# Sums of squares of the input norm taken by TensorE instead of VectorE, in a kernel of two transformer-like blocks

## The reference

```python
def rmsnorm(x, w):
    xf = x.astype(jnp.float32)
    xf = xf * lax.rsqrt(jnp.mean(xf * xf, axis=-1, keepdims=True) + EPS)
    return (xf * w.astype(jnp.float32)).astype(x.dtype)

def hybrid_layer(x, p_i, norm_pre, ...):
    h = rmsnorm(x, norm_pre)
    proj = h @ w_in
    ...
    gate = jax.nn.sigmoid(x @ w_ple_gate)
    return x + gate * (p_i @ w_ple_proj)
```

## Time and profile before

| | |
|---|---|
| runs | 2607.85, 2612.5, 2614.89 us |
| span of the profiled execution, first to last instruction | 2605.7 us |
| TensorE matmuls busy | 2510.6 us, 96% |
| VectorE busy | 1361.5 us, 52% |
| ScalarE busy | 633.4 us, 24% |
| GpSimd busy | 1034.6 us, 40% |
| mean granted clock of TensorE | 0.985 |

### The profile page before, as it was taken

The page is one execution under the profiler, slowest core; times in us unless marked ns, Lnnn a source line. Parts: engine busy times, 40 slices in busy tenths (PEclk is TensorE's granted clock), DMA queues, the critical chain, the costliest instruction groups (busy, mean ns, idle before and its releaser), DMA issues.

```text
span 2605.7 us, 34941 instructions
## 1 busy us (share of the span) xinstructions
PE 2510.6 (96%) x13322; PEld 2056.9 (79%) x13322; DVE 1361.5 (52%) x1592; ACT 633.4 (24%) x714; POOL 1034.6 (40%) x467
## 2 busy tenths in 40 slices
PE   7999999999999799999999999999899999999996
PEld 5778888887888588778778787888678888888885
DVE  6765565556511751223366666556845435445357
ACT  4332232222201211350122222221421111111113
POOL 4443433343433643233222332334444444444441
PEclk9999999998999899999999999999899999999998
DMA  5112222122111321122212222221011111111111
GB/s 197 49 58 73 73 80 73 64 89 81 41 48 60 110 89 59 64 101 77 93 62 74 78 69 73 85 97 48 25 49 49 49 48 48 48 48 49 48 49 65
DMA packets 77307, 178.40 MB, mean 68 GB/s; under 512 B 8225, under 2 KB 34081, under 8 KB 76210
## 3 DMA queue, kind: packets, MB, share of 16 engines
q1 hardware_dynamic: 36288, 119.55, 13.8%
q10 hardware_dynamic: 40946, 57.78, 6.5%
HBM read 149.98 MB, written 27.33 MB: 68 GB/s over the span
## 4 chain that ended last, share of the span: by engine, by line
PE 84%; DVE 8%; issue 3%; DMA 2%; ACT 2%; POOL 1%; ACTq 0%; DVEq 0%; POOLq 0%
PE pt L1486 71%; PE pt L1516 2%; PE pt L1502 2%; DMA eb<-o_d 1%; PE wk L1783 1%; DVE eb L1324 1%; PE wk L1641 1%; PE wk L1553 1%; PE wk L1642 1%; PE wk L1753 1%; PE wk L1818 1%; PE wk L1817 1%; PE wk L1541 1%; PE wk L1822 1%; PE wk L1705 0%
## 5 line engine op out<-in xcount | busy, mean ns | idle before, releaser
L351 POOL TENSOR_TENSOR w_hi<-w_raw,ones 128x1024 fp32r<-128x1024 f32 x202 | 390.3, 1932 | 1468.6 <-PE pt L1486 1403.5
L355 POOL TENSOR_TENSOR w_lo<-w_raw,w_hi 128x1024 fp32r<-128x1024 f32 x202 | 588.3, 2912 | 15.8
L1486 PE MATMUL pt<-h,w_hi 128*128 128x512 f32 x1376 | 439.6, 401 | 8.6 <-POOL w_lo L355 4.6
L1486 PE MATMUL pt<-l,w_hi 128*128 128x512 f32 x1376 | 426.2, 391 | 0.0
L1486 PE MATMUL pt<-h,w_lo 128*128 128x512 f32 x1376 | 425.3, 390 | 0.0
L1486 PE MATMUL pt<-xh,w_hi 128*128 128x512 f32 x976 | 305.6, 395 | 7.3 <-POOL w_lo L355 4.8
L1486 PEld LDWEIGHTS pt<-l,w_hi 128*128 128x128 f32 x1376 | 259.3, 188 | 55.7
L1486 PEld LDWEIGHTS pt<-h,w_lo 128*128 128x128 f32 x1376 | 258.9, 188 | 55.5
L1486 PE MATMUL pt<-xh,w_lo 128*128 128x512 f32 x976 | 302.7, 392 | 0.0
L1486 PEld LDWEIGHTS pt<-h,w_hi 128*128 128x128 f32 x1376 | 250.6, 189 | 64.2 <-issue 6.3
L1486 PE MATMUL pt<-xl,w_hi 128*128 128x512 f32 x864 | 269.0, 393 | 0.0
(11 more groups left out here) (355 smaller groups left out, 3314.1 us busy)
## 6 DMA issues: line engine op xcount, KB each, us to landing
w_raw<-ws_d SPq DMA_DIRECT2D x204, 512.0 KB, 3.4
x_raw<-xT_d SPq DMA_DIRECT2D x32, 256.0 KB, 7.4
rowb<-acs_d ACTq DMA_DIRECT2D x8, 1024.0 KB, 4.6
qkc<-qk_d ACTq DMA_DIRECT2D x9, 512.0 KB, 3.9
pp_d<-ebuf ACTq DMA_DIRECT2D x8, 512.0 KB, 3.3
sz_d<-eb ACTq DMA_DIRECT2D x8, 512.0 KB, 2.6
eb<-pp_d ACTq DMA_DIRECT2D x8, 512.0 KB, 4.2
qk_d<-ebuf ACTq DMA_DIRECT2D x8, 512.0 KB, 2.7
```

The source lines that it names most:

```text
L351: nc.gpsimd.tensor_tensor(out=w_hi[:, u, :], in0=w_raw[:, u, :], in1=zeros, op=ALU.add).then_inc(w_hi_done, 1)
L355: nc.gpsimd.tensor_tensor(out=w_lo[:, u, :], in0=w_raw[:, u, :], in1=w_hi[:, u, :].bitcast(f32), op=ALU.subtract).then_inc(w_split, 1)
L1486: ins = MM(pt[:, slot, h * HALF:(h + 1) * HALF], wt[:, w, k * P:(k + 1) * P], x[:, k, h * HALF:(h + 1) * HALF], start=first and k == 0 and ...
```

## The change

TensorE now sums the squares themselves, without VectorE. For each half tile q it makes four matmuls with a quarter of the squares as the stationary operand and the column of ones as the moving one, and the 8 tiles of a half accumulate in the same four columns of PSUM (bank 3 of wk for the first half, bank 2 for the second). Squares lie in six buffers: four in the space of acc_a and acc_b, and the two in ec. ScalarE waits for a buffer only from the seventh square on. The groups of four matmuls are spread over the PLE tiles: q = 0 to 3 ahead of tile 0, then 4 and 5, 6 and 7, 8 to 10, 11 to 13, 14, and 15 behind tiles 0 to 5. The spread of the first half stands behind tile 2, that of the second half behind tile 7, ahead of the projection. The last group of a half is followed by a wait of TensorE for first_acc (or sq_used), then it raises stat_done. ScalarE's table of steps and VectorE's order are new; VectorE's adds and copies are gone.

```diff
--- before.py
+++ after.py
@@ -138,6 +138,7 @@
     x_raw = at("x_raw", [KT, T], R1)
     p_raw, p_hi, p_lo = at("p_raw", [2, T], R2), at("p_hi", [2, T], R3, f32r), at("p_lo", [2, T], R3 + 8192, f32r)
     acc_a, acc_b = at("acc_a", [1024], BC), at("acc_b", [1024], BC + 4096)
+    xsq = at("xsq", [4, HALF], BC)
     acc_g = at("acc_g", [2, 1024], R3 + 24576)
 
     raw_p = at("raw_p", [2, T + CW], R2 + 8192)
@@ -230,6 +231,10 @@
     def cols(h):
 
         return slice(h * HALF, (h + 1) * HALF)
+
+    def x_square(q):
+
+        return xsq[:, q % 6, :] if q % 6 < 4 else ec[:, cols(q % 6 - 4)]
 
     def sem(name):
         return ctx.enter_context(nc.semaphore(name))
@@ -415,11 +420,9 @@
 
             h, k = divmod(q, KT)
             act.wait_ge(x_in[h][k], 16)
-            if q in (KT, KT + 1):
-                act.wait_ge(first_acc, q - 1)
-            elif q >= 2:
-                act.wait_ge((first_acc, sq_used)[h], k - 1)
-            A(ec[:, cols(q % 2)], x_raw[:, k, cols(h)], ACT.Square).then_inc((first_sq, sq_done)[h], 1)
+            if q >= 6:
+                act.wait_ge(*((first_acc, q - 5) if q < 14 else (sq_used, q - 13)))
+            A(x_square(q), x_raw[:, k, cols(h)], ACT.Square).then_inc((first_sq, sq_done)[h], 1)
 
         def embedding(k):
 
@@ -436,10 +439,10 @@
             act.wait_ge((half_val, val_done)[h], k + 1)
             A(xh[:, k, cols(h)], x_raw[:, k, cols(h)], ACT.Copy).then_inc((half_hi, hi_done)[h], 1)
 
-        for step, first, end in ((square, 0, 4), (embedding, 0, 1), (square, 4, 6), (embedding, 1, 2), (square, 6, 8),
-                                 (embedding, 2, 3), (square, 8, 10), (embedding, 3, 4), (square, 10, 12),
-                                 (embedding, 4, 5), (high, 0, 3), (square, 12, 14), (embedding, 5, 6), (high, 3, 5),
-                                 (square, 14, 16), (embedding, 6, 7), (high, 5, 8), (embedding, 7, 8)):
+        for step, first, end in ((square, 0, 6), (embedding, 0, 1), (square, 6, 8), (embedding, 1, 2), (square, 8, 11),
+                                 (embedding, 2, 3), (square, 11, 14), (embedding, 3, 4), (high, 0, 2), (square, 14, 16),
+                                 (embedding, 4, 5), (high, 2, 4), (embedding, 5, 6), (high, 4, 6), (embedding, 6, 7),
+                                 (high, 6, 8), (embedding, 7, 8)):
             for q in range(first, end):
                 step(q)
         for q in range(KT, 2 * KT):
@@ -869,23 +872,13 @@
         for k in range(2):
             dve.wait_ge(p_hi_done, k + 1)
             TT(out=p_lo[:, k, :], in0=p_raw[:, k, :], in1=p_hi[:, k, :].bitcast(f32), op=ALU.subtract).then_inc(p_lo_done, 1)
-        def half_scale(h, n):
+        def half_scale(h, n, sums=3):
 
             dve.wait_ge(stat_done, n)
             a, b = 4 * h, 4 * h + 4
-            link(TS(sm[:, 8 + a:8 + b], wk[:, 3, a:b], 1.0 / D, EPS1, ALU.mult, ALU.add))
+            link(TS(sm[:, 8 + a:8 + b], wk[:, sums, a:b], 1.0 / D, EPS1, ALU.mult, ALU.add))
             rsqrt(sm[:, a:b], sm[:, 8 + a:8 + b], sm[:, 16 + a:16 + b], rstd_done)
 
-
-        def add_square(q):
-            h, k = divmod(q, KT)
-            dve.wait_ge((first_sq, sq_done)[h], k + 1)
-            if k:
-                dve.wait_ge((first_acc, sq_used)[h], k)
-                ins = TT(out=acc_a[:, cols(h)], in0=acc_a[:, cols(h)], in1=ec[:, cols(q % 2)], op=ALU.add)
-            else:
-                ins = nc.vector.tensor_copy(acc_a[:, cols(h)], ec[:, cols(q % 2)])
-            ins.then_inc((first_acc, sq_used)[h], 1)
 
         def scaled(q):
 
@@ -902,14 +895,13 @@
             TT(out=xl[:, k, cols(h)], in0=x_raw[:, k, cols(h)], in1=xh[:, k, cols(h)].bitcast(f32),
                op=ALU.subtract).then_inc((half_lo, lo_done)[h], 1)
 
-        for q in range(KT):
-            add_square(q)
         half_scale(0, 1)
-        for step, first, end in ((add_square, 8, 12), (scaled, 0, 4), (add_square, 12, 14), (scaled, 4, 6),
-                                 (add_square, 14, 16), (scaled, 6, 8), (scaled_low, 7, 8)):
-            for q in range(first, end):
-                step(q)
-        half_scale(1, 2)
+        for q in range(5):
+            scaled(q)
+        half_scale(1, 2, 2)
+        for q in range(5, KT):
+            scaled(q)
+        scaled_low(KT - 1)
         for q in range(KT, 2 * KT):
             scaled(q)
         scaled_low(2 * KT - 1)
@@ -1560,15 +1552,25 @@
             return ins
 
         pe.wait_ge(cst, 1)
-        def first_sums(h):
-            pe.wait_ge((first_acc, sq_used)[h], KT)
-            half_sums(acc_a, 0, h).then_inc(stat_done, 1)
+        def square_sums(first, end):
+
+            for q in range(first, end):
+                h, k = divmod(q, KT)
+                pe.wait_ge((first_sq, sq_done)[h], k + 1)
+                for c in range(4):
+                    ins = MM(wk[:, 3 - h, 4 * h + c:4 * h + c + 1], x_square(q)[:, c * P:(c + 1) * P], ones[:, 0:1],
+                             start=k == 0 and c == 0, stop=k == KT - 1 and c == 3, skip_group_check=True)
+                ins.then_inc((first_acc, sq_used)[h], 1)
+                if k == KT - 1:
+                    pe.wait_ge((first_acc, sq_used)[h], KT)
+                    pe.sem_inc(stat_done, 1)
 
         def first_spread(h):
             pe.wait_ge(rstd_done, 1 + h)
             half_spread(wka, 0, h).then_inc(spread_done, 1)
 
 
+        square_sums(0, 4)
         pe.wait_ge(p_lo_done, 2)
         for n in range(KT):
             w, nt = n // 4, n % 4
@@ -1585,18 +1587,14 @@
             if nt == 3:
                 pe.wait_ge(ple_done, n + 1)
                 pe.sem_inc(mm_done, 1)
+            if n < 6:
+                square_sums(*((4, 6), (6, 8), (8, 11), (11, 14), (14, 15), (15, 16))[n])
             if n == 2:
-                first_sums(0)
-            if n == 4:
                 first_spread(0)
-
-        def in_xbc(n):
-            if n == 3:
-                first_sums(1)
-            if n == 11:
+            if n == 7:
                 first_spread(1)
 
-        pair_by_half(S_XBC, N_XBC, (xh, xl), 0, 0, in_xbc, tile_first=True)
+        pair_by_half(S_XBC, N_XBC, (xh, xl), 0, 0, lambda n: None, tile_first=True)
 
         pe.wait_ge(sml_in, 48)
         narrow(0, wdt_raw, (xh, xl)).then_inc(dt_mm, 1)
```

## The result

| | before | changed |
|---|---|---|
| median of 9 runs each, same chip | 2610.78 us (2604.82 to 2615.68) | 2619.6 us (2612.57 to 2624.03) |
| span of the profiled execution | 2605.7 us | 2610.9 us (its own time 2612.57) |
| first PLE matmul starts | 13.8 us | 17.9 us |
| narrow matmuls (L1541, now L1533) start | 69.0 us | 79.2 us |

The ratio is 1.0036, 95% interval 1.0022 to 1.0050: by it the changed kernel is slower by 9.4 us (5.7 to 13.1); the two medians differ by 8.8. The forecast was +12.1 us. The profiled execution of the changed kernel happens to be the quickest of its nine, and its span is only 5.2 us longer than that of before. Its mean granted clock is 0.986, where the nine have a median of 0.984: an estimated 5 us less lost to low clock than in the middle one.

What follows compares the result with a forecast made beforehand. TensorE was taken to bound the kernel, so delay at the narrow matmuls (69.0 us) moves the end one for one. 4.0 + 9.0 + 0.8 - 5.1 + 3.4 = +12.1 us, giving 2624.6; range 2616 to 2633.

Steps and rivals of the forecast that it cites:

- Ahead of tile 0: Before the first PLE tile: four groups at the low clock take 10.9 to 17.8, starting tile 0 4.0 us late.
- Rival 1: First stage: groups are as cheap at the low clock and it doesn't fall again; +4.7 us, 2617.2, chance 0.16.
- Ten more groups at 0.90: Between PLE tiles on TensorE: twelve groups come, two old ones go, nothing hides them; +9.0 us.
- the lower bound: For the groups between PLE tiles: 8.1 us if neighbouring groups share the restart.
- Rival 2: Between PLE tiles: groups hide under the wide matmuls, leaving only waits; -4.3 us, 2608.2, chance 0.03.
- Five waits: TensorE before 69 us: waits for acc_a, PLE tile copies (ebuf) and xl go; -5.1 us, no ebuf wait left.
- Its own sums: After each half's last group TensorE waits for its own result before stat_done; two waits, +0.8 us.
- The clock: Behind PLE tiles 2 and 3: one short fall of 3.4 us at half clock each; +3.4 us.
- rival 3: Behind PLE tiles 2 and 3: the clock stays low, a long fall at each; +18.9 us, 2631.4, chance 0.14.
- Nothing behind 69 us changes: After the narrow matmuls' start: its shift moves the end one for one; over 2 us later change means forecast wrong.
- Scaling began at 36.0 for my 35: VectorE in the first stage: scaling was to start from about 35 us, after the spread, against 34.38 before.

Runs made afterwards that it cites:

- e3: Changed kernel with 26 wide matmuls of constants on TensorE ahead of the first group; 2616.89 us, ratio 1.0023 to the kernel before.
- e4: Changed kernel with every group of four one-column matmuls done twice, the second into unused columns; 2646.39 us, ratio 1.0140 to the kernel before.
- e1: Changed kernel with the four groups ahead of PLE tile 0 moved behind it, beside groups 4 and 5; 2623.95 us, ratio 1.0056 to the kernel before.
- e2: Changed kernel with no group ahead of tile 0, groups 3, 3, 3, 3, 2, 2 behind tiles 0 to 5, first spread behind tile 3; 2622.15 us, ratio 1.0058.
- e12: Changed kernel with groups behind tiles 0 to 5 dealt two by two, four still ahead of tile 0; 2614.34 us, ratio 1.0024 to the kernel before.
- e6: Kernel before, VectorE still adding, with nine square buffers, twelve squares first, all adds before scaling, spread behind PLE tile 3; 2605.22 us, ratio 0.9989.
- e8: Changed kernel with no group ahead of tile 0, one group mid and one at end of each PLE tile, spreads moved; 2623.62 us, ratio 1.0052.
- e7: e6 with 26 wide matmuls of constants ahead of PLE tile 0; 2611.06 us, ratio 1.0004 to the kernel before.
- e10: Kernel before with nine buffers, root after ten adds, 41 wide constant matmuls up to tile 0, sums behind tile 2, spread behind 4; 2629.06 us, ratio 1.0073.

## Why the prediction was right, and where not

- **Ahead of tile 0, +4.0.** Held: 1.7 us per group, tile 0 at 17.90 for 17.8. e3 shows that it is the clock (0.89 behind wide matmuls), e4 that it adds up. Rival 1 falls. A group's eight weight loads start 0.107 us apart at the high clock (0.86 / 8) and 0.213 at the low (1.70 / 8). The rule of the Trainium skill on LDWEIGHTS ("TensorE: Matmul & The Clock Gate") gives 0.107 for 128 columns at either; the rows agree with it at the high clock alone.
- **Ten more groups at 0.90, +9.0.** Held: 1.79 us for two in a row, 2.68 for three and 0.90 for one, each with the 0.09 behind it, so the twelve take 10.8 us as reckoned. A group in a row costs 0.85 to 0.86 where a single one costs 0.81, and that takes up what the lower bound would have saved. Rival 2 falls with e4.
- **Five waits, -5.1.** Nearly: the rows show 0.3 left for ebuf, where I had written that none would be.
- **Its own sums, +0.8.** One wait of 0.3 stands in the list as such; the other, behind the last group, lies with the 0.3 put down to ebuf. Too small to tell apart.
- **The clock, +3.4.** This was the step that failed, by half: one fall of 3.4 us instead of two. The row of three groups and the spread brought it, the row of three behind tile 3 did not. With one fall the sum is 10.4; the mark says 10.2. My grounds for the term were weaker than I wrote: in both stretches of the earlier trace rows that I called nothing but groups TensorE had stood idle ahead of them, 2.59 us before 1858.47 and 3.1 us before 623.7. That rows of groups bring the clock down without an idle time is shown by e1, e2 and e3 only. e12 shows that my count could not have been exact. e1 and e2 show that rival 3, a clock that stays low, was close by: another place of the same groups loses 8.5 us more.
- **Nothing behind 69 us changes.** Wrong as I put it: I named over 2 us as a sign of error, and in the profiled run the later part gave back 5.1. TensorE's lack of idle time between 69 and 100 us said nothing of the SSD loop, where it waits 3.8 us for rowb. By the ratio (+9.4) less of it is left than in that one run. That +12.1 came so near +9.4 is in part luck: the sum itself is tested by the +10.2 at the mark, and what came behind it, which I had put at nothing, happened to come out small.
- Scaling began at 36.0 for my 35, since the spread itself runs into the fall.

## What to carry to other kernels

To move a reduction from a VectorE with time to spare to a full TensorE cost all of its time there: ask first what waits the VectorE version causes, here 4.5 us of listed waits against 13 us of matmuls (4.0 ahead of tile 0 and 9.0 behind). Price narrow matmuls at both clocks. Of the places tried here the cheapest was ahead of the first wide matmul, where the clock was low anyway: with four groups there the mark was +10.2 and +11.0, with none +14.2 to +18.3. And before a wait is moved, look at what GpSimd does at the new place, since VectorE's smallest step can stand behind it (e6).

## What I had not expected of the hardware

- Rows of one-column matmuls bring the granted clock down though TensorE is never idle: six in a row for 10.2 us (e1), three for 3.4 (changed kernel) and for 3.4 to 6.8 (e2). Sixteen dealt out singly between wide ones brought no fall, but the rise came at 25.7 instead of 17.1 us (e8).
- Executions of the same instructions on TensorE (changed kernel and e12, up to 30 us) differ in when the clock rises, 21.4 and 23.1, and in whether a row brings a fall.
- A warm-up was lost in a pause: after 3.7 us without work the matmuls were at the low level again (e7); 41 matmuls right up to the work kept the high one (e10).
- A VectorE step on 128x4 numbers takes 0.16 us, and 1.76 and 2.19 beside GpSimd's split (e6).
- A fall of the clock at another place went with a shorter stage: the first SSD pass is 3 us shorter in the ten runs whose low stretch comes at its start; that the one causes the other is read, not tested.
- TensorE can stand still in the midst of a stream for nothing that the profile shows: 9.3 us in four pauses in e10, none in before.
